# Output projections that begin with six depth steps, last down products of the second block in two parts, and modulation sums one unit later

## The reference

```
def hybrid_layer(x, ...):                                  # first block, 2 layers
    h = rmsnorm(x, norm_mix_pre)
    q, k, v, rw, gate_a, gate_b = split(h @ w_in)
    y_att = sliding_window_attention(rope(q), rope(k), v, sinks) @ w_o_att
    y_rw = rwkv7_time_mix(rw, ...) @ w_o_rw
    mixed = sigmoid(gate_a) * y_att + sigmoid(gate_b) * y_rw
    x = x + rmsnorm(mixed @ w_out, norm_mix_post)
    h = rmsnorm(x, norm_ffn_pre)
    ua, ub = split(causal_dwconv(h @ w_up, conv_w, conv_b))
    x = x + rmsnorm((gelu(ua) * ub) @ w_down, norm_ffn_post)
    return x + rmsnorm(sigmoid(x @ w_ple_gate) * (p_i @ w_ple), norm_ple)

def second_block(x, c, ...):                               # 2 layers
    for l in range(2):
        sh1, sc1, g1, sh2, sc2, g2 = split(silu(c) @ w_ada[l] + b_ada[l])
        h = rms_norm(x, ln1_g[l]) * (1 + sc1) + sh1
        u_pool, c_q, c_kv, k_rope, gz_a, gz_b = split(h @ w_in[l])
        y_a = pool_mixer(u_pool, w_pool[l], pool_scale[l]) @ p_pool[l]
        y_b = mla(c_q, c_kv, k_rope, ...) @ p_attn[l]
        merged = sigmoid(gz_a) * y_a + sigmoid(gz_b) * y_b
        x = x + g1 * (merged @ w_out[l])
        h2 = rms_norm(x, ln2_g[l]) * (1 + sc2) + sh2
        x = x + g2 * (square(relu(h2 @ w_ff1[l])) @ w_ff2[l])
    return rms_norm(x, final_g)
```

## Time and profile before

| what | value |
|---|---|
| median of 3 runs | 4149.19 us (4147.81 to 4152.53) |
| the profiled execution's own time | 4148.27 us |
| its span | 4146.5 us |
| mean granted TensorE clock | 0.97 |
| matmuls (PE) busy | 3915.7 us, 94% |
| weight loads (PEld) busy | 3201.3 us, 77% |
| DVE / ACT / POOL busy | 2163.3 / 1681.0 / 1691.7 us |
| DMA | 379.61 MB, mean 92 GB/s |

### The profile page before, as it was taken

The page is one execution under the profiler, slowest core; times in us unless marked ns, Lnnn a source line. Parts: engine busy times, 40 slices in busy tenths (PEclk is TensorE's granted clock), DMA queues, the critical chain, the costliest instruction groups (busy, mean ns, idle before and its releaser), DMA issues. The chain is left out here.

```text
span 4146.5 us, 68426 instructions
## 1 busy us (share of the span) xinstructions
PE 3915.7 (94%) x28856; PEld 3201.3 (77%) x28856; DVE 2163.3 (52%) x3026; ACT 1681.0 (41%) x2817; POOL 1691.7 (41%) x904
## 2 busy tenths in 40 slices
PE   7999988989999899998898999989999999999998
PEld 6888867877887688886687788777878887777887
DVE  6777673149865677767414986535241113523112
ACT  5554444344334454543434433435233224523222
POOL 4444412434445444441243444524434443443443
PEclk9999999989999899999998999989999999999999
DMA  3111213325543211111332554321323322122332
GB/s 131 47 49 43 68 41 115 102 81 174 183 142 97 82 47 43 49 52 61 104 102 80 174 188 142 97 72 46 97 83 97 101 92 77 48 90 89 99 97 82
DMA packets 108736, 379.61 MB, mean 92 GB/s; under 512 B 12560, under 2 KB 12944, under 8 KB 107792
## 3 DMA queue, kind: packets, MB, share of 16 engines
q1 hardware_dynamic: 98208, 357.27, 26.8%
q10 hardware_dynamic: 10224, 17.97, 1.2%
HBM read 359.46 MB, written 15.73 MB: 90 GB/s over the span
## 5 line engine op out<-in xcount | busy, mean ns | idle before, releaser
L289 POOL TENSOR_TENSOR Wlo<-raw,Whi 128x1024 fp32r<-128x1024 f32 x552 | 1375.0, 2495 | 2052.7 <-ACT Whi L276 2052.5
L224 PE MATMUL ps<-hh,Whi 128*128 128x512 f32 x2864 | 1155.4, 403 | 48.0 <-POOL Wlo L289 11.9
L224 PE MATMUL ps<-hl,Whi 128*128 128x512 f32 x2864 | 1124.7, 393 | 0.0
L224 PE MATMUL ps<-hh,Wlo 128*128 128x512 f32 x2864 | 1124.4, 393 | 0.0
L276 ACT ACTIVATE Whi<-raw 128x1024 fp32r<-128x1024 f32 x552 | 581.1, 1054 | 718.4 <-PE ps L224 598.2
L224 PEld LDWEIGHTS ps<-hh,Whi 128*128 128x128 f32 x2864 | 543.8, 190 | 184.4 <-issue 35.8
L224 PEld LDWEIGHTS ps<-hl,Whi 128*128 128x128 f32 x2864 | 544.3, 190 | 117.3 <-issue 8.6
L224 PEld LDWEIGHTS ps<-hh,Wlo 128*128 128x128 f32 x2864 | 542.7, 189 | 116.4
L224 PE MATMUL ps<-gh,Whi 128*128 128x512 f32 x864 | 339.2, 393 | 7.6 <-issue 5.7
L224 PE MATMUL ps<-gh,Wlo 128*128 128x512 f32 x864 | 337.4, 391 | 0.0
L224 PE MATMUL ps<-gl,Whi 128*128 128x512 f32 x864 | 337.4, 391 | 0.0
(11 more groups left out here) (367 smaller groups left out, 5989.4 us busy)
## 6 DMA issues: line engine op xcount, KB each, us to landing
raw<-in_stream SPq DMA_DIRECT2D x554, 512.0 KB, 3.5
ada<-in_ada SPq DMA_DIRECT2D x96, 512.0 KB, 4.2
park_x<-xT SPq DMA_DIRECT2D x2, 2048.0 KB, 7.2
park_yh<-yh ACTq DMA_DIRECT2D x16, 256.0 KB, 2.1
park_yl<-yl ACTq DMA_DIRECT2D x16, 256.0 KB, 2.3
xT<-park_x SPq DMA_DIRECT2D x2, 2048.0 KB, 8.0
yrh<-park_yh ACTq DMA_DIRECT2D x16, 256.0 KB, 8.2
yrl<-park_yl ACTq DMA_DIRECT2D x16, 256.0 KB, 8.1
```

What stands on the lines that cost most here:

```text
L224: last = pe.matmul(ps, left[a](k), right[c](k), start=start and k == 0 and i == 0, stop=stop and k == n - 1 and i == 2)
L289: pool.tensor_tensor(b["Wlo"][:, slot], b["raw"][:, raw_slot(b, u)], b["Whi"][:, slot].bitcast(F32), SUB) \
```

## The change

Three things change.

- `SUM_LAG` goes from 3 to 4: each `mods_pe` of TensorE, and the copy of the finished sums, come one FFN unit later.
- In both blocks, `mixed_high_act` and `mixed_low_dve` take a range. Tiles 0 to 5 are done in round 3, the high parts behind that round's sigmoids, the low parts ahead of its products; tiles 6 and 7 follow at the end. TensorE's wait before `project_pe` is now for the 16th sigmoid (`gate_a`) and no more for the last product (`gate_v`).
- `last_down_pe` takes the number of tiles and is used for the last part of the second block too (32 tiles: 6 depth steps, then 2). The scalar engine's list gets the matching `high.upto` ahead of the last `g_high`.

```diff
-ADA, ADA_LAG, SUM_LAG = 2, 3, 3
+ADA, ADA_LAG, SUM_LAG = 2, 3, 4
...
+def mixed_high_act(act, s, b, first, end):
+
+    act.wait_ge(s["gate_p"], 8 * 3 + 4)
+    for i in range(first, end):
+        act.wait_ge(s["gate_v"], MIX_V(i // 2, f"m{i % 2}"))
+        act.activation(b["hh"][:, i], b["mixed"][:, i], ACT.Copy).then_inc(s["mx_hi"], 1)
+
+
+def mixed_low_dve(dve, s, b, first, end):
+    for i in range(first, end):
+        dve.wait_ge(s["mx_hi"], i + 1)
+        dve.tensor_tensor(b["hl"][:, i], b["mixed"][:, i], b["hh"][:, i].bitcast(F32), SUB).then_inc(s["mx_lo"], 1)
...
@@ gated_act
             act.activation(b["sg"][:, i], b["ps"][:, i], ACT.Sigmoid).then_inc(s["gate_a"], 1)
+        if t == 3:
+            mixed_high_act(act, s, b, 0, KD - 2)
         for i in range(4, units):
             high.around(act, unit(t, i))
+    mixed_high_act(act, s, b, KD - 2, KD)
@@ gated_dve
             extra(t)
+        if t == 3:
+            mixed_low_dve(dve, s, b, 0, KD - 2)
         for i in range(4):
...
             dve.tensor_tensor(out[:, 2 * t + j], b["sg"][:, j], b["sg"][:, 2 + j], ADD).then_inc(s["gate_v"], 1)
+    mixed_low_dve(dve, s, b, KD - 2, KD)
@@ last_down_pe
-    g = PART * (PARTS1 - 1)
-    n, early = FT - g, FT - g - 2
+    parts = -(-tiles // PART)
+    g = PART * (parts - 1)
+    n, early = tiles - g, tiles - g - 2
...
-            i = KD * (PARTS1 - 1) + m
+            i = KD * (parts - 1) + m
@@ first block and second_pe, ahead of project_pe
-                    pe.wait_ge(s["gate_v"], MIX_V(3, "b1"))
+                    pe.wait_ge(s["gate_a"], 16)
@@ second_pe
+        elif key[1] == PARTS2 - 1 and key[2] < OPEN:
+            if key[2] == 0:
+                last_down_pe(pe, s, b, ring, FT2)
@@ second_act
             if i == FT2 - 1:
+                high.upto(act, AT2_FFN + FFN2[1][("down", PARTS2 - 1, OPEN - 1)] + 1)
                 g_high(i)
```

More of the change, by code:

```diff
@@ L1836, in ffn_pe, with last_down_pe @@
         elif key[2] == 0:
-            last_down_pe(pe, s, b, ring)
-def last_down_pe(pe, s, b, ring):
-    g = PART * (PARTS1 - 1)
-    n, early = FT - g, FT - g - 2
+            last_down_pe(pe, s, b, ring, FT)
+def last_down_pe(pe, s, b, ring, tiles):
+    parts = -(-tiles // PART)
+    g = PART * (parts - 1)
+    n, early = tiles - g, tiles - g - 2
     held = []
@@ L2133, in _ @@
                     gated_act(act, s, b, high, lambda t, i: AT_GATE + 8 * t + i, 8, sines)
-                    mixed_high_act(act, s, b)
                     def square_y(m):
@@ L2174, in _ @@
                               lambda t: angle_steps(dve, s, b, "tb2", "freq2", list(ANGLE.at)[(0, 5, 9, 15)[t]:(5, 9, 15, 15)[t]]))
-                    mixed_low_dve(dve, s, b)
                     for i in range(1, KD - 2):
```

## The result

The changed kernel takes 4122.94 us (median of 4 runs, 4121.95 to 4125.17) beside 4150.64 us (4147.81 to 4152.53) before: ratio 0.9935, 95% interval 0.9923 to 0.9946. That is faster by 27.7 us, by the interval 22 to 32. The profiled execution took 4125.17 us with a span of 4123.3, that is 23.1 us under the one before; the forecast for this pair was 23.7.

What follows compares the result with a forecast made beforehand. TensorE, busy 3915.7 of 4146.5 us, bounds the kernel, so gains come from gaps or half clock. Terms 12.2 + 3.2 + 3.7 + 1.4 + 3.2 = 23.7 us gave a forecast of 4125.5 us, range 4120 to 4130.

Steps and rivals of the forecast that it cites:

- Projections, 4 x 3.04 us: Output projections, four places: TensorE's stall after the last gate matmul goes, 3.04 us each, 12.2 us in all.
- cover of 1.3 us in the second block: Second block's projection: low weight pieces still finish 1.3 us before TensorE wants them, so no new wait.
- Rival 2: Second block: weights come late at two projections and the fourth down unit, 6.1 + 3.7 us less gain, 4135.3; chance 0.08.
- What the rule on SBUF would have cost: Output projections: early low parts meet GpSimd's weight pieces; one may lose about 2.2 us, and the sum stays.
- Last down products, 2 x 1.87 us: Second block's last down part, two places: 3.09 us won less 1.22 at the fourth unit, 3.7 us in all.
- The fourth unit's wait: Second block's last down part: a new wait for the low weight piece, 1.11 us and 0.11 of start-up.
- Sums a unit later, 1.4 us: First block's FFN, two layers: waits on macc move to the low weight piece, leaving 0.7 us a layer.
- Rival 3: First block's FFN: vector engine does not set the pace, macc waits go for good, 18.5 us, 4108.4; chance 0.04.
- The clock, 6.4 us: Half-clock falls go: 3.2 us behind two output projections and 3.2 us in the first block's FFN.
- The four named falls: Falls at 836.03, 3723.71 (projections), 1177.37 and 2532.46 (first block's FFN) go, 1.6 us each.
- The count of half-clock stretches: Whole kernel: the prediction is wrong if the number of half-clock stretches stays at what it is.
- The prediction's reserve: Every later stage: a shifted start can move other half-clock stretches by one or two of 1.6 us, either way.

Runs made afterwards that it cites:

- e8: The changed kernel with two weight units held together instead of three in the second block's last part: 4125.23 us, ratio 0.9935 to the kernel before.
- e4: The changed kernel with the modulation sums back at a lag of three units (SUM_LAG 3): 4126.86 us, ratio 0.9946 to the kernel before.
- e3: The kernel before with only the modulation sums one unit later (SUM_LAG 4): 4151.61 us, ratio 1.0007 to the kernel before.
- e6: The changed kernel with each modulation add cut to 64 of 512 columns, lag 4: 4105.24 us, ratio 0.9886 to the kernel before.
- e7: The changed kernel with each modulation add cut to 64 of 512 columns and lag 3: 4103.69 us, ratio 0.9886 to the kernel before.
- e12: The changed kernel with modulation pieces mostly beside down units, two weight units held in the second block's last part, lag 4: 4109.41 us, ratio 0.9896 to before.

## Why the prediction was right

The forecast was 4125.5 us, with 4120 to 4130 as its own range, and the time is 4122.94. By its own steps:

- **Projections, 4 x 3.04 us:** right. From the last gate matmul to the first projection matmul each place wins 2.96 or 2.97 us, and 3.04 to the second where no fall lies over it: 12.2. The order that was worked out (low parts ahead of the first product, last low part 4.6 us early, cover of 1.3 us in the second block) came out to within 0.2 us each. Rival 2 is out.
- **What the rule on SBUF would have cost:** nothing, and here the case didn't test it. The Trainium skill's page "SBUF — State Buffer", section "Who interferes with whom", gives the lock-out; the trace has the six early low parts in 3.70 us, none stretched (682 to 694 ns in all 32), since GpSimd had nothing to do at that moment. The prediction had them meet its weight pieces, and overlooked what it says itself a few lines above: the piece is queued behind the six high parts. GpSimd starts it at 817.47, 0.10 us before the sixth low part ends, and it is so at all four places. What such a meeting costs elsewhere in this kernel is in the last section.
- **Last down products, 2 x 1.87 us:** right, 2.0 each. The fourth unit's wait was read off the first block's row, 1.34 us from start to start, and came as 1.36. e8 shows that it hangs on the three units held.
- **Sums a unit later, 1.4 us:** right in mechanism, somewhat less in size: 0.2 and 0.3 us in the first stretches and 0.2 behind the second ones, 0.9 in all, or 1.1 by e4 against the kernel after. Alone it made no measurable difference (e3). The waits did move to the low weight piece, the vector engine's cadence stayed at 24.0 us, and e6 and e7 show that the lag is worth nothing once that engine isn't behind. Rival 3 is out.
- **The clock, 6.4 us:** right at the edited places, by luck in the sum. The four named falls went, and they are 6.3 us of the table. That a fall goes with its break is borne out by all traces together (12 of 18 with the stall, none of 66 without it). How many falls a given execution of before has is chance, two behind these six stalls here and six in e3, so 3.2 us for the stalls is what this one trace had and not what they cost on average; by 12 of 18 the six would bring four falls, 6.4 us, an estimate. The count of half-clock stretches, the prediction's sign of being wrong, fell from 28 to 25. Other falls came, in stages without an edit: 150 of the 128x512 matmuls start in half clock before, and 150 after. The prediction's reserve (other stretches by one or two of 1.6 us, either way) was needed, and it happened to cancel.

That the total came out at 23.1 beside 23.7 is therefore in part luck: the steps at edited places were right by their mechanisms, and the rest added up to nothing.

Of the medians' 27.7 us the traces account for 23.1. The profiled execution of the kernel after is the slowest of its four runs (4125.17), and the one of before lies 2.4 us under its median of 4150.64, which is the other 4.6 us: the spread of runs. One source of it, of some us, is in the last section; whether it makes these 4.6 is not shown.

Left open: of the 3.9 us between the medians of e4 and the kernel after, the traces put 1.1 down to the sums; the rest would be the clock elsewhere or the spread of runs, and the intervals overlap. Also open is how much of the vector engine's lateness in the first block's FFN is its work and how much its meetings with GpSimd, since every run that lightened or moved the one changed the other too.

## What to carry to other kernels

Before you take a wait away, ask whether the engine waited for sets the pace of its stage. If it is idle there, the wait goes for good (the projections and the last down part, 3.0 us a place, of which the last down part gives 1.1 back at another wait). If it is busy nearly all the time (22.14 of 24.00 us), the wait only turns up under another name, and what helps is to move its work to units where it has room (e12, 16 us more by the ratios). Where a split reduction holds weight slots to fill a stall, count what the next unit waits for its slot, and hold no more than the stall needs.

## What the runs showed of the hardware

**The clock.** The same break in TensorE's work, a wait of 2.8 us, was followed by 3.4 us (once 6.8) at the 1.2 GHz level in two of six places in one profiled execution and in six of six in another, of kernels with the same code there. Over all traces it is 12 of 18, and none of 66 at the same places without the break. Each 3.4 us costs 1.6 us where TensorE sets the pace, and nothing that lasts where the vector engine does (e4). Over all fourteen profiled executions the time at half clock lies between 218 and 271 us of the span in 22 to 33 stretches. It isn't ordered by how many stalls a kernel has left: the most belongs to e3 (270.8 us), which has fewer waits on `macc` than before (245.3). A difference of a few us between two traces of this kernel can't be put down to an edit unless it is seen at the edited place and without the clock, or in many traces.

**Two instructions that start together.** Near 49 us, ahead of everything edited, a vector instruction and a weight piece of GpSimd start at nearly the same time. DVE and POOL of the kernel after:

```profile
49.05 2.95 DVE L1336 SCALAR_TENSOR_TENSOR ar<-dz,par,zp 128x512 f32<-128x512 f32 x1
49.06 2.39 POOL L289 TENSOR_TENSOR Wlo<-raw,Whi 128x1024 fp32r<-128x1024 f32 x1 [1.81 <-ACT Whi L276]
```

and of the kernel before:

```profile
48.90 0.75 DVE L1336 SCALAR_TENSOR_TENSOR ar<-dz,par,zp 128x512 f32<-128x512 f32 x1
49.01 2.88 POOL L289 TENSOR_TENSOR Wlo<-raw,Whi 128x1024 fp32r<-128x1024 f32 x1 [1.91 <-ACT Whi L276]
```

This meeting is in both layers of the first block, so 28 times in the fourteen traces. In the ten where the vector engine was ahead of GpSimd by 0.016 us or less, or behind it, its instruction took 2.87 to 2.95 us and the piece 2.37 to 2.39; in the 18 where it was ahead by 0.048 us or more, 0.75 us and 2.74 to 2.94. TensorE then waits for `lol` for 3.3 us instead of 1.9, and a fall of the clock followed in 8 of the ten and in 2 of the 18. In the kernel after the vector engine was not far enough ahead in either layer, in before it was in both, and the falls at 54.8 and 1406.5 stand right behind these longer waits. So each layer of this execution bore 1.5 us of wait and 1.6 us of half clock that hung on some hundredths of a us between two starts, in stages without an edit.
